# Latent attention of a streaming encoder: the eight query tiles of a head run in the order 0, 7, 1, 6, 2, 5, 3, 4

## What is computed

```python
s = (jnp.einsum('bqhc,bkc->bhqk', q_lat, ckv)
     + jnp.einsum('bqhr,bkr->bhqk', q_rope, krope)).astype(jnp.float32) * ((NOPE + ROPE_DIM) ** -0.5)
mask = (kpos[None, :] // CHUNK) <= (qpos[:, None] // CHUNK)      # CHUNK = 64
p = jax.nn.softmax(jnp.where(mask, s, NEG_INF), axis=-1)
o_lat = jnp.einsum('bhqk,bkc->bqhc', p.astype(ckv.dtype), ckv)
...
o = jnp.einsum('bthc,chd->bthd', o_lat, w_uv)                    # then * silu(g), then @ w_out
```

## Time and profile before

| | us |
|---|---|
| median of 3 runs (1816.11 to 1824.68) | 1822.04 |
| the profiled execution | 1824.61 |
| its span | 1822.8 |
| granted TensorE clock, mean share | 0.958 |
| latent attention, first score to last `mix` copy | 1364.46 to 1696.2 |

### The profile page before, as it was taken

How to read it: one execution, slowest core, us unless ns; L and a number is a source line. 1 busy time by engine, 2 the same in 40 slices (tenths; PEclk the granted TensorE clock), 3 DMA queues, 4 the chain that set the end, 5 groups by cost and what they waited for, 6 DMA issues and landing times. The chain is left out here.

```text
span 1822.8 us, 34118 instructions
## 1 busy us (share of the span) xinstructions
PE 1658.0 (91%) x12822; PEld 1297.1 (71%) x12822; DVE 1263.3 (69%) x2750; ACT 806.9 (44%) x1777; POOL 227.2 (12%) x314
## 2 busy tenths in 40 slices
PE   4788999999999969989998989998969999999798
PEld 1575577778888847767776878787857677767687
DVE  2577577779988938778887646437437777777764
ACT  3447322221112137768873326312217677767321
POOL 2222000000001032010100000110024232220000
PEclk7799999999999979999998989999989999999899
DMA  8314247652333169998727533424242111111532
GB/s 315 79 39 108 85 128 208 197 168 95 96 106 112 50 164 247 236 215 218 197 92 254 225 130 105 127 61 135 69 107 58 29 29 31 35 29 45 186 123 96
DMA packets 212243, 229.26 MB, mean 126 GB/s; under 512 B 122265, under 2 KB 146433, under 8 KB 211058
## 3 DMA queue, kind: packets, MB, share of 16 engines
q1 hardware_dynamic: 205202, 207.17, 40.5%
q0 software_dynamic: 6880, 19.92, 2.9%
HBM read 169.72 MB, written 54.16 MB: 123 GB/s over the span
## 5 line engine op out<-in xcount | busy, mean ns | idle before, releaser
L905 PE MATMUL PS<-ab_wh,hT 128*128 128x512 f32 x576 | 231.6, 402 | 3.8 <-DVE ab_wl L1256 3.8
L906 PE MATMUL PS<-ab_wl,hT 128*128 128x512 f32 x576 | 226.1, 392 | 0.0
L907 PE MATMUL PS<-ab_wh,hT 128*128 128x512 f32 x576 | 225.5, 392 | 0.0
L1449 DVE TENSOR_SCALAR_CACHE_REDUCE topk_junk<-scores,topk_small 128x528 bf16<-128x528 f32 (+6 forms) x224 | 194.6, 915 | 1.3
L2661 DVE CUSTOM_DVE_ANT_0 la_S<-PS,la_mask 128x128 f32<-128x128 f32 (+3 forms) x144 | 107.5, 747 | 41.7 <-PE PS L907 28.5
L1214 ACT ACTIVATE ab_nat<-PS 128x512 f32<-128x512 f32 x54 | 32.2, 596 | 229.9 <-PE PS L907 229.9
L905 PEld LDWEIGHTS PS<-ab_wh,hT 128*128 128x128 f32 x576 | 108.6, 189 | 31.5 <-issue 5.8
L907 PEld LDWEIGHTS PS<-ab_wh,hT 128*128 128x128 f32 x576 | 108.5, 188 | 24.8
L906 PEld LDWEIGHTS PS<-ab_wl,hT 128*128 128x128 f32 x576 | 108.6, 189 | 21.5
L905 PE MATMUL PS<-out_wh,out_mT 128*128 128x512 f32 x288 | 116.2, 404 | 4.7 <-DVE out_mT L2111 4.7
L1808 ACT ACTIVATE at_P<-at_S,at_nm 128x128 f32<-128x128 f32 (+2 forms) x144 | 110.5, 767 | 16.7 <-DVE at_nm L1853 16.3
(11 more groups left out here) (428 smaller groups left out, 4223.6 us busy)
## 6 DMA issues: line engine op xcount, KB each, us to landing
ab_wl_raw<-in_ab_w_in SPq DMA_DIRECT2D x64, 256.0 KB, 5.1
spare<-in_ada_w SPq DMA_DIRECT2D x32, 512.0 KB, 4.1
out_g<-scratch_gates_nat SPq DMA_DIRECT2D x18, 512.0 KB, 5.3
at_vc<-in_cache_a_v SPq DMA_DIRECT2D x8, 1024.0 KB, 10.4
at_vc<-in_cache_b_v SPq DMA_DIRECT2D x8, 1024.0 KB, 5.5
scratch_qcT<-c_T SPq DMA_DIRECT2D x72, 96.0 KB, 2.0
mod_ada_w<-in_ada_w SPq DMA_DIRECT2D x6, 1024.0 KB, 10.4
c_wl_raw<-in_c_w_in SPq DMA_DIRECT2D x24, 256.0 KB, 5.9
```

The lines of the kernel that those rows point to most:

```text
L905: nc.tensor.matmul(out, x[0], w[0], start=start, stop=False)
L906: nc.tensor.matmul(out, x[0], w[1], start=False, stop=False)
L907: return nc.tensor.matmul(out, x[1], w[0], start=False, stop=stop)
L1449: go(V.tensor_scalar(mark, x, limit, 0.0, op, ALU.add, accum_out=cnt[:, m:m + 1]), 0 if m == M - 1 else 1)
```

## The change

The tiles of a head run in the order 0, 7, 1, 6, 2, 5, 3, 4. The batch tile keeps its place, the fifth of a head (the ninth in head 0). `TILES.index(i)` takes the place of i in all counters and in the choice of the weight buffer. The first places that need half 0 and half 1 of k and v are now tiles 0 and 7, so the waits for the expansion stand there. Since tile 7 is second, the two k units come first in the prologue (both in iteration -2), the two v units after them (both in iteration -1). The `mix` copy follows tile 4.

```diff
+    TILES = [0, 7, 1, 6, 2, 5, 3, 4]
     order = []
     for g in range(HC):
-        for i in range(QT):
+        for n, i in enumerate(TILES):
             order.append(("head", g, i))
-            if i == (QT - 1 if g == 0 else 3):
+            if n == (QT - 1 if g == 0 else 3):
                 order.append(("batch", g, QT))
+    FIRSTS = (0, 7)
-    tiles_done = lambda g, i: QT * g + i + 1
+    tiles_done = lambda g, i: QT * g + TILES.index(i) + 1
...
-    for n, (kind, half) in enumerate((("k", 0), ("v", 0), ("k", 1), ("v", 1))):
-        early[FIRST + n].append((kind, 0, half))
+    for n, (kind, half) in enumerate((("k", 0), ("k", 1), ("v", 0), ("v", 1))):
+        early[FIRST + n // 2].append((kind, 0, half))
     for a in range(1, NA):
-        early[head_at(2 * a - 2, 2)].append(("k", a, 0))
-        early[head_at(2 * a - 2, 6)].append(("k", a, 1))
-        early[head_at(2 * a - 1, 2)].append(("v", a, 0))
-        early[head_at(2 * a - 1, 5)].append(("v", a, 1))
+        early[head_at(2 * a - 2, TILES[2])].append(("k", a, 0))
+        early[head_at(2 * a - 2, TILES[6])].append(("k", a, 1))
+        early[head_at(2 * a - 1, TILES[2])].append(("v", a, 0))
+        early[head_at(2 * a - 1, TILES[5])].append(("v", a, 1))
...
-                    sp.wait_ge(scored, head_at(g - 2, QT - 1) + 1)
+                    sp.wait_ge(scored, head_at(g - 2, TILES[-1]) + 1)
...
-                if i in (0, 4) and g % 2 == 0:
+                if i in FIRSTS and g % 2 == 0:
                     pe.wait_ge(expanded, expanded_at(("k", g // 2, i // 4)))
...
-                if i in (0, 4) and g % 2 == 0:
+                if i in FIRSTS and g % 2 == 0:
                     pe.wait_ge(expanded, expanded_at(("v", g // 2, i // 4)))
-                if i == 0 and g:
+                if i == TILES[0] and g:
                     pe.wait_ge(resulted, g)
-                hs, cols = QT * g + i, slice(DV * (g % 2), DV * (g % 2 + 1))
+                hs, cols = QT * g + TILES.index(i), slice(DV * (g % 2), DV * (g % 2 + 1))
...
-                if 0 <= it - 1 < N and order[it - 1][0] == "head" and order[it - 1][2] == QT - 1:
+                if 0 <= it - 1 < N and order[it - 1][0] == "head" and order[it - 1][2] == TILES[-1]:
                     g = order[it - 1][1]
-                    dve.wait_ge(valued, tiles_done(g, QT - 1))
+                    dve.wait_ge(valued, tiles_done(g, TILES[-1]))
```

More of the change, by code:

```diff
@@ L2377, in _ @@
                     if a >= 2 and half == 0:
-                        pool.wait_ge(scored, head_at(2 * a - 3, QT - 1) + 1)
+                        pool.wait_ge(scored, head_at(2 * a - 3, TILES[-1]) + 1)
                     cols = slice(half * 512, (half + 1) * 512)
@@ L2385, in _ @@
                     if a >= 2 and half == 0:
-                        pool.wait_ge(valued, tiles_done(2 * a - 3, QT - 1))
+                        pool.wait_ge(valued, tiles_done(2 * a - 3, TILES[-1]))
                     hi, lo = (v[:, a % 2, d, 4 * half:4 * half + 4, :].rearrange("p a b -> p (a b)") for d in range(2))
@@ L2442, in score_head @@
                 to = 2 * (s % 2)
-                if i == 0:
+                if i == TILES[0]:
                     pe.wait_ge(head_in[g % 2], (64 if g % 2 else 32) * (g // 2 + 1))
@@ L2586, in _ @@
                     kind, g, i = order[it]
-                    hs = QT * g + i
+                    hs = QT * g + (TILES.index(i) if kind == "head" else 0)
                     if kind == "head" and hs >= 2:
```

## The result

The changed kernel takes 1825.15 us (median of 20 runs), the kernel before on the same chips 1821.2 (20 runs): ratio 1.003, 95% interval 1.0017 to 1.0042. The medians differ by +3.95 us where +4.3 was predicted; the interval of the ratio stands for +3.1 to +7.6 us. So the change costs a little, clear of the noise, and stays within the 0.5% that I called no change.

What follows compares the result with a forecast made beforehand. PE's queue was taken to set the pace, waiting practically only for lo on DVE. Pairs +2.1, opening +1.7 and head 14 +0.5 summed to +4.3 us: 1826.3 against the median, 1828.9 against the profile; range 1813 to 1840.

Steps and rivals of the forecast that it cites:

- the sum of gaps: PE's waits in one pair of heads of the kernel before, added from start to start: 4.55 us.
- The tile table: Tile-by-tile sum of PE cover against DVE's lo in each head: waits 4.85 against 4.55, +0.30 us a pair.
- The opening: Start of the stage, head 0: net +1.7 us, bounds 0.65 won and +5.
- The bank wait at `ql`: Head 0, loaded iterations of tiles 7 and 6: bank rotation makes `ql` wait for lo(7), put at 0.7 us.
- V(B)'s 0.7: Head 0: the batch tile's value product waits 0.7 us because its copy is behind max(7').
- The second bank wait: Head 0, loaded iterations of tiles 7 and 6: the second of two waits there, put at 0.9 us.
- The early k unit: Opening: the second k unit runs in PE's idle time, 1.3 us won; v half 1 coming earlier costs 0.65.
- rival 2: Slip at tile 7: V(7) waits about 0.6, T(6) and V(6) 0.3 more each head; 1840 us; chance 0.24, wholly or half.
- the walk of the end: Last head: V(2), a 1.13 wait, T(3), V(5), four `o` jobs, V(4); 19.9 us from the last `mix` copy but one.
- Rival 1: Faster by hiding: V(4) and tile 5's bank wait do not bite, DVE having caught up; 1808 to 1812 us, chance 0.12.
- Rival 3: The waits are merely moved and sum to the same, +0 to +4 us; chance 0.62 together with the forecast.
- Rival 4: The granted clock falls after longer waits, some +3 us; chance 0.02 together with something unseen in the opening.

Runs made afterwards that it cites:

- e4: The changed kernel with tile order 2, 4, 6, 7, 5, 3, 0, 1, a ramp up and down: 1797.87 us, ratio 0.9887 to the kernel before.
- e8: Tile order 3, 7, 6, 5, 0, 1, 2, 4, tile 4 last as in the changed kernel: 1793.31 us, ratio 0.9848 to the kernel before.
- e3: The changed kernel with DVE running lo(4) ahead of max(7') in the iteration of tile 4: 1838.84 us, ratio 1.0108 to the kernel before.
- e7: The changed kernel with DVE's lo copy of `kr` cut from 512 to 8 columns, outputs wrong: 1822.28 us, ratio 1.0007 to the kernel before.
- e6: The changed kernel with the batch tile behind the last tile of every head, its dependent jobs moving too: 1836.54 us, ratio 1.0086 to the kernel before.
- e1: The kernel before, tiles 0 to 7, with both k units in iteration -2 and both v units in -1: 1818.4 us, ratio 0.9989.
- e5: The kernel before, tiles 0 to 7, with the batch tile behind the last tile of every head, dependent jobs moving too: 1799.47 us, ratio 0.9887.

## Why the prediction was right

**The bound and the mechanism.** Right. PE's queue sets the pace, and all that moved is its waits on lo. e4 and e8 show how far that goes: a pair with practically no brackets takes 36.55, so 3.8 us of each pair of before could be had, where the sum of gaps said 4.55. Most of the other 0.75 is still there as short waits without a bracket: from start to start, four of 0.13 to 0.17 in e4's pair and three of 0.23 to 0.28 in e8's, among them the 0.22 shown above.

**The tile table.** Each line can be read in the trace. The predicted waits run from start to start; a bracket is about 0.16 shorter.

| step | predicted, from T's start | measured |
|---|---|---|
| V(7) | 2.83, no wait | 1495.28 to 1498.11: 2.83, none |
| V(6) | 2.63, wait 0.16 | 1499.30 to 1501.93: 2.63, no bracket; 0.16 from start to start |
| unit behind T(5) | 2.15, wait 1.13 | even head bracket 1.11, some 0.2 of it a missing matmul; odd head 0.88; from start to start 1.05 each |
| V(4) behind an even head | 2.29, wait 0.98 | 2.38, bracket 0.88, wait 1.05 |
| V(4) behind an odd head | wait 1.29 | bracket 1.35, wait 1.52 |
| V(0) to V(3) | none | none |
| the pair | +0.30 | +0.30, six pairs +0.32 each |

The PE rows for V(7) and V(6), with T(7), T(1) and T(6) ahead:

```profile
1495.28 1.04 PE L2486 MATMUL PS<-ident,la_P 128*128 128x128 f32 x8
...
1497.86 0.42 PE L2486 MATMUL PS<-ident,la_P 128*128 128x128 f32 x2
1498.11 0.19 PE L905 MATMUL PS<-la_v,la_PT 128*128 128x64 bf16 x1
...
1499.30 0.93 PE L2486 MATMUL PS<-ident,la_P 128*128 128x128 f32 x7
...
1501.93 0.19 PE L905 MATMUL PS<-la_v,la_PT 128*128 128x64 bf16 x1
```

The one line that is off by more than 0.1 is V(4) behind an odd head, 0.23 too low; the two units are 0.08 too high each. (The prediction's own 2.29 less 1.34 gives 0.95 for V(4), not 0.98.)

**The reason given for V(4)'s wait** was half wrong. I named the widest maximum ahead of lo and the short jobs behind T(4) together. e3 takes the maximum away and the wait of 0.9 stays; e8 keeps it, gives PE work, and the wait goes, but for 0.22 behind an odd head. The table's own line had it: hi allows no lo before 1.32, and the maximum ended at 1.34. Only what the `kr` copy adds was DVE's load: 0.31 in the table, 0.47 in e7.

**The opening.** The size is near, in part by luck. The bank wait at `ql` that I put at 0.7 is there with 0.66, and V(B)'s 0.7 is there as 0.66. The second bank wait, put at 0.9, is not there: no other bracket of PE in head 0 is above 0.23. In its place stands one that I had not listed, 0.84 at the first v unit of head 1. In head 0 B stands behind the last tile, so its turn back follows T(7) of head 1 and takes a bank, and the v unit needs the bank of the first half of T(7), as in e6. PE's timeline, in order `ql`, the value product of B and that v unit:

```profile
1370.63 0.23 PE L905 MATMUL PS<-la_qs,la_ukT 64*128 64x128 bf16 x1 [0.66 <-DVE la_PT L2681]
...
1389.12 1.13 PE L2508 MATMUL PS<-la_lat,la_PTs 128*128 128x128 f32 x8 [0.66 <-DVE la_PTs L2675]
...
1393.81 0.23 PE L905 MATMUL PS<-la_us,la_latT 128*128 128x128 bf16 x1 [0.84 <-DVE la_PT L2681]
```

The early k unit, 1.3 less the 0.65 for v, comes to 0.43 in e1. The parts of the stage must be read with care here. The first `mix` copy lies within V(B)'s wait, so heads 0 and 1 share it. And S(7'), eight blocks, now runs ahead of that copy where S(1'), two blocks, did: at 0.1625 for each block, 0.98 us of head 0's 1.68 is work that came forward. The second copy has five blocks more ahead of it, and head 15 has five less, 0.81 us. Heads 0 and 1 lost 2.63 together; without these 0.81, and with the 0.23 that any odd head wins, the opening cost some 2.05 where 1.7 stood, an estimate from these numbers.

**Head 14 and the end.** Head 14 is an even head and belongs to the seventh pair. Its +1.02 is the 0.53 of any even head and 0.49 more, as forecast (0.5). The end is what the sum had wrong: +0.42 from copy to copy, where nothing stood, although head 15 holds 0.81 us less work than before. Its waits are thus some 1.2 longer, an estimate from these two numbers. One of them is V(7)'s:

```profile
1679.49 0.19 PE L905 MATMUL PS<-la_v,la_PT 128*128 128x64 bf16 x1 [0.41 <-DVE la_PT L2681]
```

Heads 14 and 15 have no k or v unit behind T(7). For that case rival 2 itself says 0.6; from start to start it is 0.57, and for head 15 the walk of the end does not list it.

**The sum.** The stage grew by 5.97 in the two traces: pairs 2.2 (2.1 predicted), head 14 0.5 (0.5), the end 0.4 (0), heads 0 and 1 beyond an ordinary odd head 2.9 (1.7). Of the last difference 0.8 is the work that came forward, which the terms of the opening leave out and the end, taken from copy to copy, already has as a gain. So the stage says +6 where the sum says +4.3. The medians differ by 3.95. Both 4.3 and 5.97 lie within the interval of 3.1 to 7.6, so the nearness of 3.95 to 4.3 is partly luck, and the runs cannot tell the two apart.

**The column for PE's busy time** was foretold near 37 and is 36.22. It counts modelled ends: with fewer and longer stalls there is less modelled tail, missing records take some 0.4 more, and e4, e5 and e8, nearly without stalls, show 36.1 to 36.2 for the same instructions. So 37.15 in the earlier trace rows was partly wait.

**The rivals.** Rival 1, faster by hiding, did not come. The Trainium skill, Perfetto Trace Analysis, Optimization Strategy, says that performance may be improved by interleaving regimes between which the most-contended engine changes. This case's traces do not bear that out for wide and narrow tiles: the alternation cost 0.3 us a pair. Rival 2, slip at tile 7: lo(7) ended 2.61 after T(7) started, with the 0.14 PE could go at 2.75 against 2.83; the 0.08 of slack held wherever a k or v unit follows, and not in heads 14 and 15. Rival 3, the same waits at other places, is what came. Rival 4, clock: waits with brackets up to 1.35 leave the granted clock at 1.00.

What the prediction did not see is how near a faster kernel was: the ceiling of 1.9% that it gave for any reordering was real, and 1.5% of it was had by an order of the same tiles (e8) and 1.1% by moving B and the jobs placed by it (e5).

## What to carry to other kernels

In a software pipeline over several engines, write down for each tile how long the chain through the other engines takes (here 2.1 to 2.8 us from T over hi and lo) and how much work the bounding engine has in its own program between the chain's start and its first user, and count bank or buffer reuse as a user. Choose the order so that this work outlasts the chain at every wide tile, count which unit the bank rotation makes each job wait for, as a small unit between two jobs (here B's turn back) changes it, and put large independent pieces (here B) where the count is short; alternation of wide and narrow does neither by itself. Moving an instruction of the second engine ahead is worth nothing when its own input has not landed.

## What the runs showed of the hardware

- The chain, start to start, was the same in every kernel: hi 0.69 after the first transpose of a wide tile, lo 1.32 to 1.33 after it at the earliest, PE 0.14 to 0.15 after lo ends.
- PE's waits, with brackets of 0.9 to 1.35 us, two in a head, did not lower the granted clock: 1.00 in all windows of pairs.
- In the opening of the changed kernel, where the granted clock of the window 1354 to 1364.4 is 0.59, matmuls of 128 columns start 0.107 us apart (1359.26 to 1359.37, and so on); later, at a granted clock of 1.00, 0.055.
